# Two mixture-of-experts layers with 32 wide experts: the last pair's down product by column halves, and the layer norm's statistics moved into the expert stage

## The reference

```python
for layer in range(2):
    mix = even_mixer(...) if layer % 2 == 0 else fourier_mixer(x, w_out_fourier)
    x = layer_norm(DEEPNORM_ALPHA * x + mix, ln1_gain[layer], ln1_bias[layer])
    ffn = hierarchical_moe_2(x, ...)        # below
    x = layer_norm(DEEPNORM_ALPHA * x + ffn, ln2_gain[layer], ln2_bias[layer])
...
gate = jax.nn.softmax(top_val, axis=-1) * p_group            # two experts of 32 for each token
hid = jax.nn.silu(lax.ragged_dot(xs, w_gate, sizes)) * lax.ragged_dot(xs, w_up, sizes)
ys = lax.ragged_dot(hid, w_down, sizes) * gate.reshape(-1)[order][:, None]
out = jax.ops.segment_sum(ys, tok, num_segments=T)
```

## Time and profile before

| | us |
|---|---|
| median of 3 runs (lowest, highest) | 1913.22 (1911.63, 1914.84) |
| the profiled execution | 1919.44 |
| its span, first to last instruction | 1917.7 |
| TensorE busy in it | 1800.0 (94%) |
| VectorE busy | 704.7 (37%) |
| ScalarE busy | 399.0 (21%) |

### The profile page before, as it was taken

The page is one execution under the profiler, slowest core; times in us unless marked ns, Lnnn a source line. Parts: engine busy times, 40 slices in busy tenths (PEclk is TensorE's granted clock), DMA queues, the critical chain, the costliest instruction groups (busy, mean ns, idle before and its releaser), DMA issues. The chain is left out here.

```text
span 1917.7 us, 20705 instructions
## 1 busy us (share of the span) xinstructions
PE 1800.0 (94%) x8560; PEld 934.7 (49%) x8560; DVE 704.7 (37%) x1395; ACT 399.0 (21%) x671; POOL 75.7 (4%) x63
## 2 busy tenths in 40 slices
PE   7999999998999998999999999998799999999885
PEld 6884445794555554455533444333255434443331
DVE  3557774345334334453322222112423222222124
ACT  2421332341321222231211111111111111111111
POOL 0000001511000000210000000000000000000000
PEclk9999998899999999999999999999898999999998
DMA  5343432008399993654899999999797999999995
GB/s 208 133 165 132 148 116 48 1 1 360 116 422 406 414 411 137 248 195 169 331 424 423 424 423 425 424 425 425 281 422 293 425 423 424 423 424 424 424 424 232
DMA packets 95521, 583.45 MB, mean 304 GB/s; under 512 B 19323, under 2 KB 21499, under 8 KB 30397
## 3 DMA queue, kind: packets, MB, share of 16 engines
q1 hardware_dynamic: 90669, 580.43, 74.0%
q10 hardware_dynamic: 4752, 1.61, 0.4%
HBM read 578.83 MB, written 3.15 MB: 303 GB/s over the span
## 5 line engine op out<-in xcount | busy, mean ns | idle before, releaser
L1792 PE MATMUL up_ps_l<-pool,hT 128*64 128x512 f32 x576 | 129.2, 596 | 11.1 <-DMA pool<-in_expert_w_up 11.1
L426 PE MATMUL proj_ps<-pool,hT 128*128 128x512 f32 x320 | 138.3, 592 | 0.0
L1792 PE MATMUL gate_ps_l<-pool,hT 128*64 128x512 f32 x576 | 128.9, 594 | 7.8 <-DMA pool<-in_expert_w_gate 7.7
L1813 PE MATMUL y_ps_l<-pool,hidden_l 128*64 128x512 f32 x576 | 129.2, 596 | 4.2 <-ACT hidden_l L1882 2.4
L1951 DVE SCALAR_TENSOR_TENSOR y_low_l<-y_ps_l,slot_gate_l,y_high_l 128x512 fp32r<-128x512 f32 x64 | 47.1, 751 | 195.4 <-ACT y_high_l L1892 195.4
L418 PE MATMUL proj_ps<-hT,pool 128*128 128x256 f32 x512 | 111.9, 380 | 0.0
L418 PEld LDWEIGHTS proj_ps<-hT,pool 128*128 128x128 f32 x512 | 96.9, 190 | 14.8 <-issue 1.8
L1941 DVE TENSOR_TENSOR hidden_l<-hidden_l,up_ps_l 128x512 f32<-128x512 f32 x32 | 22.0, 688 | 220.1 <-PE up_ps_l L1792 220.1
L426 PEld LDWEIGHTS proj_ps<-pool,hT 128*128 128x128 f32 x320 | 60.8, 190 | 74.4 <-issue 74.1
L1892 ACT ACTIVATE y_high_l<-y_ps_l,slot_gate_l 128x512 fp32r<-128x512 f32 x64 | 44.0, 688 | 206.4 <-PE y_ps_l L1813 202.8
L1792 PEld LDWEIGHTS gate_ps_l<-pool,hT 128*64 128x64 f32 x576 | 40.4, 137 | 93.4 <-issue 75.4
(11 more groups left out here) (531 smaller groups left out, 2731.4 us busy)
## 6 DMA issues: line engine op xcount, KB each, us to landing
pool<-in_expert_w_up SPq DMA_DIRECT2D x36, 2048.0 KB, 32.0
pool<-in_expert_w_down SPq DMA_DIRECT2D x36, 2048.0 KB, 32.1
pool<-in_expert_w_gate SPq DMA_DIRECT2D x36, 2048.0 KB, 32.2
pool<-in_w_in_blocks SPq DMA_DIRECT2D x18, 2048.0 KB, 7.6
gate_room<-in_expert_w_gate SPq DMA_DIRECT2D x14, 2048.0 KB, 27.0
store<-in_expert_w_up SPq DMA_DIRECT2D x14, 2048.0 KB, 23.9
pool<-in_moe_w_gate SPq DMA_DIRECT2D x12, 2048.0 KB, 12.3
pool<-in_moe_w_up SPq DMA_DIRECT2D x12, 2048.0 KB, 11.8
```

The costliest lines, as they stand in the source:

```text
L426: last = mm(pp[:, n % 2, j * W:(j + 1) * W], k.hT[:, c, j * P:(j + 1) * P], wbuf[n % 2][:, c, :], start=(c == 0), stop=(c == KC - 1))
L1792: last = mm(out[e * CAP:(e + 1) * CAP, 0:H], xg(part * r + c)[:, 0, at:at + CAP], ex.weights(i, e, c), start=(part + c == 0), stop=(part = ...
L1813: last = mm(Y[e * CAP:(e + 1) * CAP, n], hidT[:, part * r + c, e * CAP:(e + 1) * CAP], ex.weights(i, e, c)[:, n * W:(n + 1) * W], start=(p ...
```

## The change

Three things are changed, all in the wide expert stages (of two parts) and in the norm behind them.

`Experts.by_columns` is true for the down weights of the last pair. There a part holds all four row groups of both experts, and 512 of the 1024 columns. It is loaded by two transfers, one for each expert, whose pieces in HBM are 2 KB long; `transfers` and `landed` count 16 for each. `last_down` takes the place of `down` for that pair: column half 0 in full from the first chunk, then half 1 from the second, then the scatters of half 0 (behind the first remainder) and those of half 1 (behind the second). VectorE does both remainders, then the additions of half 0 (`last_add`), then those of half 1.

Behind the last addition VectorE computes the norm's four BN_STATS into `k.stats`, which lives for the whole program; the general stage does the same at its end. `stage_norm` keeps BN_AGGR and what follows it.

```diff
-                    for n in range(2):
-                        o(nc.vector.bn_stats(stats[:, j, n], k.x[:, j, n * W:(n + 1) * W]))
-                    o(nc.vector.bn_aggr(mv[:, j], stats[:, j].rearrange("p n s -> p (n s)")))
+                    o(nc.vector.bn_aggr(mv[:, j], k.stats[:, j].rearrange("p n s -> p (n s)")))
...
+    def by_columns(self, p, what):
+        return self.parts == 2 and p == NE // 2 - 1 and what == 2
+
+    def transfers(self, i):
+        what, _ = self.of_pair[i % len(self.of_pair)]
+        return [0, 1] if self.by_columns(i // len(self.of_pair), what) else [slice(0, 2)]
...
-            sp.dma_start(self.places[i % room].rearrange("p (e c n) -> p e c n", e=2, c=r),
-                         self.views[what][:, 2 * pair:2 * pair + 2, part * r:(part + 1) * r]).then_inc(
-                             self.s_landed[i % room], 16)
+            rows = self.views[what][:, 2 * pair:2 * pair + 2, part * r:(part + 1) * r]
+            if self.by_columns(pair, what):
+                r, rows = self.HT, self.views[what][:, 2 * pair:2 * pair + 2, :, part * W:(part + 1) * W]
+            to = self.places[i % room].rearrange("p (e c n) -> p e c n", e=2, c=r)
+            for e in self.transfers(i):
+                sp.dma_start(to[:, e], rows[:, e]).then_inc(self.s_landed[i % room], 16)
...
+                def last_down(p):
+                    for n in range(2):
+                        i = p * CP + 2 * ex.parts + n
+                        pe.wait_ge(*ex.landed(i))
+                        for c in range(HT):
+                            for e in range(2):
+                                last = mm(Y[e * CAP:(e + 1) * CAP, n], hidT[:, c, e * CAP:(e + 1) * CAP],
+                                          ex.weights(i, e, c), start=(c == 0), stop=(c == HT - 1))
+                                if n == 0 and e == 0 and c == HT - 1:
+                                    last.then_inc(ex.s_used, 1)
+                        last.then_inc(s_y if n == 0 else ex.s_used, 1)
+                    pe.wait_ge(s_one, NI)
+                    pe.wait_ge(s_add, 4 * NI - 4)
+                    for n in range(2):
+                        pe.wait_ge(s_ys, 2 * p + n + 1)
+                        scatter(p, n)
+                        scatter(p, 2 + n)
...
+                def last_add(p, n):
+                    for j in range(NJ):
+                        dve.wait_ge(s_sc, 4 * p + 2 * n + j + 1)
+                        xs = k.x[:, j, n * W:(n + 1) * W]
+                        nc.vector.scalar_tensor_tensor(out=xs, in0=xs, scalar=1.0, in1=scatter_bank[2 * j + n],
+                                                       op0=ALU.mult, op1=ALU.add).then_inc(s_add, 1)
...
+                    if ex.by_columns(p, 2):
+                        low(p, 0)
+                        low(p, 1)
+                        last_add(p, 0)
+                        last_add(p, 1)
+                        dve.wait_ge(s_add, 4 * NI)
+                        for j in range(NJ):
+                            for n in range(2):
+                                nc.vector.bn_stats(k.stats[:, j, n], k.x[:, j, n * W:(n + 1) * W])
```

More of the change, by code:

```diff
@@ L1318, in stage_norm @@
         g, b = (k.carve(k.gate_room, NJ * 3 * T + n * D, [P, D]) for n in range(2))
-        stats = k.sb(f"stats_{tag}", [P, NJ, 2, 6])
         mv, v, inv, rs = (k.sb(f"{n}_{tag}", [P, NJ, 2]) for n in ("mean_var", "var_eps", "inv", "rstd"))
@@ L1647, in counts_after @@
         return self.used0 + self.total, [
-            n + (16 * len(range(m, self.total, self.room)) if m < self.room else 0)
+            n + (16 * sum(len(self.transfers(i)) for i in range(m, self.total, self.room)) if m < self.room else 0)
             for m, n in enumerate(self.landed0)]
@@ L1662, in weights @@
         r = self.rows(what)
+        if self.by_columns(i // len(self.of_pair), what):
+            r = self.HT
         return self.places[i % self.room].rearrange("p (e c n) -> p e c n", e=2, c=r)[:, e, c]
+    def by_columns(self, p, what):
[3 more added lines that the diff above has]
+        return [0, 1] if self.by_columns(i // len(self.of_pair), what) else [slice(0, 2)]
     def landed(self, i):
-        return self.s_landed[i % self.room], self.landed0[i % self.room] + 16 * (i // self.room + 1)
+        return self.s_landed[i % self.room], self.landed0[i % self.room] + 16 * (
+            i // self.room + len(self.transfers(i)))
     def load(self, sp, n):
@@ L1854, in _ @@
                     pe.wait_ge(s_hts, p + 1)
[L1855 to L1860, removed]
+                    if ex.by_columns(p, 2):
+                        last_down(p)
+                    else:
+                        down(p)
+                if not ex.by_columns(NI - 1, 2):
+                    pe.wait_ge(s_ys, 2 * NI)
+                    pe.wait_ge(s_one, NI)
+                    pe.wait_ge(s_add, 4 * NI - 4)
+                    for o in range(4):
+                        scatter(NI - 1, o)
             @block.scalar
@@ L1917, in add, with low @@
                                                        op0=ALU.mult, op1=ALU.add).then_inc(s_add, 1)
+                def low(p, n):
+                    dve.wait_ge(s_yh, 2 * p + n + 1)
+                    nc.vector.scalar_tensor_tensor(
+                        out=yl[:, n], in0=Y[:, n], scalar=slot_gate[:, 0:1], in1=yh[:, n].bitcast(F32),
+                        op0=ALU.mult, op1=ALU.subtract).then_inc(s_ys, 1)
+                def last_add(p, n):
[4 more added lines that the diff above has]
+                                                       op0=ALU.mult, op1=ALU.add).then_inc(s_add, 1)
                 def overflow():
@@ L1956, in _ @@
                         gated(p + 1)
-                add(NI - 1, 0, 4)
+                if not ex.by_columns(NI - 1, 2):
+                    add(NI - 1, 0, 4)
     k.scope = k.ctx
@@ L2085, in _ @@
                 dve.wait_ge(s_y, 4 * NE + 4)
+                if H == H2:
+                    for j in range(NJ):
+                        for h in range(2):
+                            nc.vector.bn_stats(k.stats[:, j, h], k.x[:, j, h * W:(h + 1) * W])
     k.scope = k.ctx
@@ L2605, in build @@
         k.count = k.sb("largest_count", [P, 1])
+        k.stats = k.sb("stats_of_x", [P, NJ, 2, 6])
         ex = [Experts(k, None, "one", H1, 4, 4, i["moe_w_gate"][0], i["moe_w_up"][0], i["moe_w_down"][0])]
```

## The result

The changed kernel is slower, and by more than was forecast: a median of 1925.46 us over 6 executions (1916.5 to 1928.66) against 1911.31 us over 6 of before (1906.68 to 1914.84), a ratio of 1.0071 with a 95% interval of 1.0043 to 1.0098. The forecast, 1917.7 with a range up to 1920.6, had the direction and about a third to a half of the size.

The account below looks back on a forecast made before the run. The weights' stream was taken to set the pace, with the serial tail mattering. Per layer -0.80 (columns), +0.5 (loads), +2.57 (statistics) and 0 (norm) gave +2.27, +4.5 in all: 1913.22 + 4.5 = 1917.7 us, range 1914.0 to 1920.6.

Parts of the forecast that it names:

- What bounds the kernel: Wide expert stages: the weights' stream sets the pace, the diff touches its last 4 MB only, so the tail matters.
- Columns: Last pair's down weights: column half 0 overlaps half 1, so the last addition ends sooner, -0.80 us a layer.
- The shape of the loads: Last two chunks of down weights: pieces of 2 KB land later, +0.5 us a layer, between 0 and +1.1.
- Statistics: End of each wide stage: four BN_STATS behind the last addition, hidden by nothing, +2.57 us a layer.
- The norm: Norm behind each layer: losing 2.8 us of VectorE work gains 0, because the bias row or TensorE's filler holds it.
- Sum of the tails: End of each wide stage: -0.80 + 0.5 + 2.57 = +2.27 us a layer, +4.5 us in all.
- rival 2: Layer 1's first products: shifted phases spare TensorE's low clock, so +4.5 becomes +1.3 us, 1914.5; chance 0.12.
- the dear end of the tail: Both tails: statistics 2.87 and pieces +1.1 make +3.17 us a layer, +6.3 in all, 1919.6; chance 0.13.
- the pieces weren't free: Last down weights: the rival that 2 KB pieces cost nothing, +1.77 us a layer, +3.5 in all, 1916.7; chance 0.17.
- the norm gave nothing back: Both norms: the rival that the moved 2.8 us of statistics cancel there, -1.1 us in all, 1912.1; chance 0.04.

Follow-up runs that it names:

- columns only: The kernel before with the last down weights by column halves, statistics still in the norm and no new allocation: ratio 0.9987.
- the run with early rows: The changed kernel with the norm's gain and bias rows loaded behind the last weights instead of at the norm's start: ratio 1.0016 to before.
- Room only: The kernel before with the 96 bytes of stats_of_x allocated in each partition but used by nothing: ratio 1.0003.

## Why the prediction was wrong

**What bounds the kernel**: right. The stream sets the pace, and the last instruction of VectorE ends the stage. But I took that as a reason to look at the tail alone. If a stream of 421 us sets the pace twice, then a change of its rate by two thousandths is worth as much as the columns' gain of 0.8 us.

**Columns**: -0.80 was forecast, -0.91 measured between the second products and the last addition.

**The shape of the loads**: +0.5 was taken from the w_in_even rows, with 0 and +1.1 as ends. Measured +0.76 and +0.88 in the changed kernel, +0.72 and +0.49 in columns only: inside the ends, nearer to the dear one in the changed kernel. The rule of the Trainium skill, "DMA: Bandwidth & Descriptors", Specifications, that 512 B or more suffice for line rate, doesn't hold here to that precision: in the last stretch of 2 KB pieces the rate was 385 to 390 GB/s. The pieces' length, their stride and the number of transfers changed together, so that the length is the cause isn't shown.

**Statistics**: +2.57 was forecast, 2.47 for the four and about 0.05 for the wait measured. The spacing taken from the additions was right (0.59 from start to start).

**The norm**: 0 twice, right both times. Behind layer 1 the wait of 3.69 us in the trace shows it, and the run with early rows, where the 3.7 us came back; behind layer 0 the Fourier products start 14.40 us after the issue of the bias row, and started 14.46 after it before.

**Sum of the tails**: +2.27 a layer was forecast, +2.34 and +2.45 measured. Up to here the working stood, though its closeness is in part luck: the pieces cost 0.3 more than I took, and the columns gained 0.1 more and the statistics took 0.05 less.

**The step that failed** stands in the first paragraph, where the prediction says that the diff touches the weights' stream "in its last 4 MB only". It put the rest of the stream at nothing without a reason: the sum has no term for the line that allocates stats_of_x, though the diff shows it. It moves gate_room and first_room off a multiple of 256 bytes and costs 2.4 to 2.8 us a layer, as much as all that I had added up. Room only shows it without any other part of the change (423.51 and 423.68 us against 420.87 and 421.10), and the landings show it load by load. The addresses can be worked out from the sizes of the tensors before a run: x 1920, pool 18304, store 116608, gate_room 150272 and first_room 183040 before; the last two 96 more after. The Trainium skill, "DMA: Bandwidth & Descriptors", How a descriptor splits into AXI transactions, says that a transaction must start at a multiple of 256 bytes, and that a descriptor which doesn't start there fetches bytes it doesn't use, which cost beats. It says this of what a transaction reads; here the sources in HBM stayed, and the destinations in SBUF moved, so no run shows that this is the mechanism. The runs have the same step of 256 (64, 96 and 128 beside it all gave 423.7).

**The rivals.** The clock (rival 2) happened in the trace: layer 1 was spared its low stretch and got 4.55 us back. But the control with before itself moved as much (SyncE restarted 6.6 us earlier), and over twelve executions the changed kernel has no higher mean clock than before (0.9818 against 0.9824). Whether the change moves the low stretches isn't settled: all four traces of kernels with both of its parts have the full clock in layer 1's first products, and one of the two traces of before has. The prediction's sum for this rival is also a little off: 4.5 less 3.4 is 1.2 with the unrounded terms, not 1.3. The other rivals fell: the dear end of the tail wasn't reached, the pieces weren't free, the norm gave nothing back.

**The range** was too narrow for a second reason. The three executions of before lay within 3.2 us, and I took that as the noise, though the profiled one was 4.6 us above the highest of them; over 69 executions of before on one chip they reach from 1899.8 to 1920.1, so that medians of six differ by some us by themselves. The first ratio, 1.0071, is above the 1.0048 and the sum of parts of 1.0053, and both lie within its interval. The six executions of the changed kernel behind it had a mean clock of 0.9797, the later twelve 0.9818; by the fit that is 3.2 us of the 4.85 between their medians. The clocks of the six of before aren't on record.

## What to carry to other kernels

Where a stream of loads sets the pace, a new tensor is part of the change even if nothing slow uses it: work out where the loads' destinations start in a partition, before and after, and keep them at a multiple of 256 bytes. Work that is moved out of a stage gains only if nothing else holds that stage; look first for what its first instructions wait for, and move that load. Cutting a last step in halves gains only what the second half doesn't already cover, and the halves' transfers have shorter pieces.

## What the runs showed of the hardware

- The start of a transfer's destination in a partition matters at a step of 256 bytes. With 11 places off a multiple of it, 8 KB pieces flow at 421 GB/s; with 8 off at 424; with 3 or none at 427. Shifts of 64, 96 and 128 bytes beside a multiple cost the same. A single load of 2 MB takes 0.12 or 0.13 us longer into a place off a multiple (4.97 instead of 4.84 us for first_room), but the mean of all loads was no lower than 4.92 in any run, with none or three places off.
- Pieces of 2 KB in HBM, at a stride of 4 KB: 0.5 to 0.9 us more for the last 4.19 MB than in pieces of 8 KB (9.9 us at 424 GB/s); the number of transfers changed with it.
- TensorE's granted clock falls in other places in each execution of the same kernel, mean clocks of 0.975 to 0.989 among the executions, each 0.001 going with 1.5 us. A difference of 5 us is better read from a stretch of the trace that has the full clock on both sides (the streams agree to 0.3 us between executions) than from medians of a dozen executions.
- BN_STATS of 128x512 float32: four without waits between them take 2.47 us, a pair with a wait between takes 1.42.
